# Fused two-block decoder on one core: memory normed in rows, cross-attention blocks interleaved with its heads, differential and sparse attention reordered

## What is computed

```python
# first block
x = x + 0.5 * swiglu(rms_norm(x, ffn1_norm), ...)
x = x + token_mixing(rms_norm(x, mix_norm), ...)          # ends in ... @ w_out
x = x + memory_cross_attention(rms_norm(x, xattn_norm), rms_norm(mem, mem_norm), w_q, w_kv, w_o)
x = x + 0.5 * swiglu(rms_norm(x, ffn2_norm), ...)

def memory_cross_attention(h, m, w_q, w_kv, w_o):         # 512 tokens, 256 memory rows, 4 heads of 256
    q = to_heads(h @ w_q, XATTN_HEADS)
    k, v = (to_heads(t, XATTN_HEADS) for t in jnp.split(m @ w_kv, 2, axis=-1))
    s = jnp.einsum('bhsd,bhmd->bhsm', q, k)
    p = jax.nn.softmax(s * (XATTN_HEAD_DIM ** -0.5), axis=-1)
    return einsum('bhsm,bhmd->bhsd', p, v) reshaped @ w_o

# diff_attention: 8 heads of two 64-wide halves, chunk-causal mask, four query tiles each
p = jax.nn.softmax(jnp.where(mask, s, -jnp.inf), axis=-1)
a = p[:, :, 0] - lam * p[:, :, 1]                         # then a @ v, rms_norm, @ w_out

# dsa_attention: 16 heads of 64, keys chosen per query by an 8-head index score
score = jnp.einsum('bqh,bqhk->bqk', wb, jax.nn.relu(dots))
vals, idx = lax.top_k(score, topk)                        # topk = 128 of up to 512
s = jnp.einsum('bqhd,bqkhd->bhqk', qb, kg); p = softmax(...)
```

## Time and profile before

| | |
|---|---|
| Time, three runs | median 2615.61 us (2611.15 to 2618.03) |
| The profiled execution | 2619.21 us, its span 2617.2 us |
| Granted TensorE clock, mean | 0.962 of full speed |
| TensorE busy | 93% of the span |
| GpSimd, ScalarE, VectorE busy | 43%, 33%, 32% |
| Bytes moved | 210.65 MB, mean 80 GB/s |

### The profile page before, as it was taken

How to read it: one execution, slowest core, us unless ns; L and a number is a source line. 1 busy time by engine, 2 the same in 40 slices (tenths; PEclk the granted TensorE clock), 3 DMA queues, 4 the chain that set the end, 5 groups by cost and what they waited for, 6 DMA issues and landing times.

```text
span 2617.2 us, 27065 instructions
## 1 busy us (share of the span) xinstructions
PE 2444.0 (93%) x11184; PEld 1970.7 (75%) x11184; DVE 845.6 (32%) x1441; ACT 863.4 (33%) x1255; POOL 1124.2 (43%) x918
## 2 busy tenths in 40 slices
PE   7999998898886999999998789999998979999999
PEld 6888876687764788888885477888875757788887
DVE  3222106463123222210455724112045955420211
ACT  4222224221432322221444534213245353431331
POOL 6444433523631544444352236445454711444442
PEclk8999999899899999999898899999999979999999
DMA  4332222212410233322221013233221200232322
GB/s 129 98 98 99 97 97 68 65 52 77 145 65 16 81 97 97 97 97 97 81 81 64 1 49 97 97 97 97 97 77 56 89 1 17 81 97 97 97 97 81
DMA packets 148588, 210.65 MB, mean 80 GB/s; under 512 B 6122, under 2 KB 116979, under 8 KB 148467
## 3 DMA queue, kind: packets, MB, share of 16 engines
q1 hardware_dynamic: 148466, 208.93, 24.6%
HBM read 206.82 MB, written 2.10 MB: 80 GB/s over the span
## 4 chain that ended last, share of the span: by engine, by line
PE 79%; DVE 10%; ACT 4%; POOL 3%; issue 2%; DMA 1%; SPq 0%; ACTq 0%; POOLq 0%; DVEq 0%
PE ps L1254 24%; PE ps L1256 23%; PE ps L1255 23%; POOL wlo L720 2%; PE ps L1879 2%; POOL sq L733 1%; DVE c_work L2542 1%; PE ps L1855 1%; DVE c_best L2541 1%; ACT whi L815 1%; DVE small L2406 1%; ACT d_p L1067 1%; PE ps L1865 1%; PE ps L1543 1%; PE ps L1308 1%
## 5 line engine op out<-in xcount | busy, mean ns | idle before, releaser
L720 POOL TENSOR_TENSOR wlo<-raw,whi 128x512 fp32r<-128x512 f32 x776 | 1011.6, 1336 | 1320.9 <-ACT whi L815 1320.9
L815 ACT ACTIVATE whi<-raw 128x2048 fp32r<-128x2048 f32 (+1 forms) x195 | 371.1, 1904 | 769.1 <-DMA raw<-in_mlp_w 326.2
L1254 PE MATMUL ps<-hh,whi 128*128 128x512 f32 x1512 | 599.6, 397 | 24.6 <-DVE hl L1984 17.3
L1256 PE MATMUL ps<-hh,wlo 128*128 128x512 f32 x1512 | 592.9, 392 | 0.0
L1255 PE MATMUL ps<-hl,whi 128*128 128x512 f32 x1512 | 592.7, 392 | 0.0
L1254 PEld LDWEIGHTS ps<-hh,whi 128*128 128x128 f32 x1512 | 286.7, 190 | 99.0 <-issue 33.6
L1256 PE MATMUL ps<-gh,wlo 128*128 128x512 f32 x864 | 336.1, 389 | 0.0
L1254 PE MATMUL ps<-gh,whi 128*128 128x512 f32 x864 | 336.1, 389 | 0.0
L1255 PE MATMUL ps<-gl,whi 128*128 128x512 f32 x864 | 336.1, 389 | 0.0
L1255 PEld LDWEIGHTS ps<-hl,whi 128*128 128x128 f32 x1512 | 287.1, 190 | 60.0 <-issue 1.5
L1256 PEld LDWEIGHTS ps<-hh,wlo 128*128 128x128 f32 x1512 | 286.3, 189 | 60.5
(11 more groups left out here) (406 smaller groups left out, 2669.9 us busy)
## 6 DMA issues: line engine op xcount, KB each, us to landing
raw<-in_mlp_w SPq DMA_DIRECT2D x64, 1024.0 KB, 5.5
raw<-in_ffn_w_gate SPq DMA_DIRECT2D x22, 1024.0 KB, 5.1
raw<-in_ffn_w_up SPq DMA_DIRECT2D x22, 1024.0 KB, 5.1
raw<-in_ffn_w_down SPq DMA_DIRECT2D x22, 1024.0 KB, 4.8
raw<-in_w_in SPq DMA_DIRECT2D x13, 1024.0 KB, 5.1
raw<-in_diff_w_in SPq DMA_DIRECT2D x12, 1024.0 KB, 5.0
raw<-in_xattn_w_kv SPq DMA_DIRECT2D x8, 1024.0 KB, 5.6
raw<-in_dsa_w_in SPq DMA_DIRECT2D x8, 1024.0 KB, 5.1
```

Of the source, the lines that this page charges most:

```text
L720: nc.gpsimd.tensor_tensor(wlo[i][:, c], raw[i][:, c], whi[i][:, c].bitcast(F32), ALU.subtract).then_inc(s_lo, 1)
L815: nc.scalar.activation(whi[i][:, 0:width(made[0])], raw[i][:, 0:width(made[0])], ACT.Copy)\
L1254: nc.tensor.matmul(dst, w_hi, x_hi, start=start, stop=False)
L1256: return nc.tensor.matmul(dst, w_lo, x_hi, start=False, stop=stop)
```

## The change

**Cross-attention.** The memory is loaded behind the first block of the mixer's out-projection, normed in rows on ScalarE (two squares with a running sum, two scaled copies of 128 x 1024) between two weight preparations, and turned by TensorE in two groups of eight transposes between out-projection blocks 0, 1 and 2. The tokens are no longer normed before the queries: `hh`, `hl` are made from `xT` times the gain, tile by tile as the out-projection's sums arrive, GpSimd adds the squares (`x_sums`), and the token's factor goes into the scale of the exponent (`xqr`). The blocks' order is `X_ORDER`; scores, turns and weighing stand between blocks. The result has buffers of its own (`x_oh`, `x_ol`), so that `hh` and `hl` are free for the next entry. The norm N_X is gone, and the indices of the entries are shifted.

**Differential attention.** The bank pair of a unit is `slot(u)`, scores and exponents of unit 0 move ahead of the last half group of the projection, VectorE does `weights(u + 1)` before `max_(u + 3)`, and the out-projection does the first six feature tiles of blocks 0 and 1 before the last two heads' outputs are turned.

**DSA.** The squares of the query rows are two of 128 x 2048 after the index-score loop, where before there were eight of 128 x 512 beside the copies; VectorE has four rounds of `top(1)` ahead of the first `stats`, and the rotations stand between rounds 10 of `top(3)` and its last six.

```diff
+X_ORDER = ("k0", "k1", "q0", "k2", "q1", "k3", "q2", "v0a", "v0b", "q3", "v1a", "v1b")
+        def slot(u):
+            return (u + 2) % 3
 # SyncE
-                    sp.wait_ge(s_x, 8 * at["x"][1])
+                    load(b, up_src(wdram["w_out"])(0))
+                    sp.wait_ge(s_mvar, GH)
                     sp.dma_start(x_mrow[:, :, :], ...)
...
 # TensorE, end of the mixer
-                project_out(b + MIX_BLOCKS, upd, lambda k: (s_mfin, k + 1), m_hi, m_lo)
+                out_part(b + MIX_BLOCKS, 0, (s_mfin, 1), m_hi, m_lo)
+                pe.wait_ge(s_xmn, MT)
+                turn_memory(0)
+                out_part(b + MIX_BLOCKS, 1, (s_mfin, 1), m_hi, m_lo)
+                pe.wait_ge(s_xml, 4)
+                turn_memory(4)
...
 # ScalarE, out-projection of the mixer and after
+                prep_to(o + 1)
+                act.wait_ge(s_memrow, 16)
+                for m in range(MT):
...
+                    nc.scalar.activation(sq[...], x_mrow[:, m, :], ACT.Square,
+                                         accum_out=xmr[:, m:m + 1]).then_inc(s_xmsq, 1)
+                act.wait_ge(s_xmvar, 1)
+                rsqrt(xmr[:, 4:6], xmr[:, 2:4], s_xmrstd)
+                act.wait_ge(s_xmr, 1)
+                for m in range(MT):
+                    nc.scalar.activation(x_mrow[:, m, :], x_mrow[:, m, :], ACT.Copy, scale=xmr[:, 4 + m:5 + m])
+                prep_to(o + 2)
...
 # VectorE, differential attention
                 weights(0)
-                weights(1)
                 for u in range(32):
-                    if u < 30:
-                        weights(u + 2)
+                    if u < 31:
+                        weights(u + 1)
                     if u < 29:
                         max_(u + 3)
 # TensorE, its out-projection
+                    out_part(out, 0, (s_dhl, 1), o_h, o_l, 0, 6)
+                    out_part(out, 1, (s_dhl, 1), o_h, o_l, 0, 6)
                     turn_out(6, 32)
                     turn_out(7, 32)
 # VectorE, DSA
                 turned_by(0, c_rowa)
+                top(1, 0, 4)
                 stats(1, c_sq0, G_Q0)
                 stats(2, c_sq1, G_Q1)
-                top(1)
+                top(1, 4)
                 stats(3, a_sq, G_K1)
                 top(2)
+                top(3, 0, 10)
                 turned_by(1, c_rowb)
                 turned_by(2, c_rowc)
-                top(3)
                 turned_by(3, c_rowa)
+                top(3, 10)
```

More of the change, by code:

```diff
@@ L457, in two_blocks @@
         s_csum = sem("s_csum")
+        s_csq = sem("s_csq")
         s_cny = sem("s_cny")
@@ L1041, in diff, with exponents @@
                 act.wait_ge(s_rr, 1)
+                def exponents(u):
+                    nk = P * (u % 4 + 1)
+                    act.wait_ge(s_dmax, u + 1)
+                    if u >= 3:
+                        act.wait_ge(s_da, u - 2)
+                    for c in range(2):
+                        k = 2 * slot(u) + c
+                        nc.scalar.activation(d_p[:, u % 3, c, 0:nk], ps[:, k, 0:nk], ACT.Exp,
+                                             bias=small[:, k:k + 1], scale=-1.0, accum_out=small[:, 12 + k:13 + k])\
+                            .then_inc(s_de, 1)
                 for g in range(6):
@@ L1087, in high @@
                         .then_inc(s_dh, 1)
-                for u in range(3):
+                for u in range(1, 3):
                     exponents(u)
@@ new lines, in xattn @@
+                pe.wait_ge(s_x, x0 + 2)
+                keys(0)
+                pe.wait_ge(s_x, x0 + 4)
+                keys(1)
+                pe.wait_ge(s_eacc, acc_at(E_X) + 7)
+                pe.wait_ge(s_x, x0 + 8)
+                for st in range(ST):
+                    r = nc.tensor.matmul(ps[:, 7, 2 * st:2 * st + 2], sq[:, 0, ts(st, P)], ones[:, 0:2],
+                                         start=True, stop=True)
+                r.then_inc(s_ess, 1)
+                queries(0)
@@ new lines, in xattn @@
+                pe.wait_ge(s_xk, 2)
+                keys(2)
+                pe.wait_ge(s_ehalf, E_X + 1)
+                scores(0)
+                pe.wait_ge(s_xk, 4)
+                queries(1)
+                pe.wait_ge(s_xk, 6)
+                keys(3)
+                scores(1)
+                queries(2)
+                pe.wait_ge(s_xk, 8)
+                values(0, 0)
+                pe.wait_ge(s_xe, 4)
+                scores(2)
+                values(0, 1)
+                queries(3)
@@ new lines, in xattn @@
+                pe.wait_ge(s_xv, 2)
+                values(1, 0)
+                pe.wait_ge(s_xe, 8)
+                scores(3)
+                pe.wait_ge(s_xe, 12)
+                turn(0)
+                values(1, 1)
+                turn(1)
+                weigh(0)
+                turn(2)
+                pe.wait_ge(s_xe, 16)
+                weigh(1)
+                turn(3)
+                weigh(2)
+                weigh(3)
+                out = b + X_BLOCKS
+                pe.wait_ge(s_xv, 4)
@@ L1566, in row_group @@
+                out_part(out, 0, (s_xol, 1), x_oh, x_ol, 0, 6)
+                out_part(out, 0, (s_xol, 1), x_oh, x_ol, 6, KT)
+                for j in range(1, OUT_BLOCKS):
+                    out_part(out, j, (s_xol, 1), x_oh, x_ol)
             def row_group(b, r0, xh, xl, kt, wcols, blocks, ready=None):
@@ L1621, in diff, with scores @@
                 half_group(b + 1, 0, 1, (2, 3))
+                def scores(u):
+                    h, qt = divmod(u, 4)
+                    if u == 0:
+                        pe.wait_ge(s_rtc, 16)
+                    if u >= 3:
+                        pe.wait_ge(s_de, 2 * (u - 3) + 2)
+                    for c in range(2):
+                        rows = slice(64 * c, 64 * c + 64)
+                        r = nc.tensor.matmul(ps[:, 2 * slot(u) + c, 0:P * (qt + 1)],
+                                             a_qT[rows, h, ts(qt, P)], a_kT[rows, h, 0:P * (qt + 1)],
+                                             start=True, stop=True)
+                    r.then_inc(s_ds, 1)
                 for g in range(1, 6):
@@ L2534, in dsa, with top @@
                 dv.link(V.memset(c_bias[0:CH, P - CH:P], -NEG))
-                def top(qt):
+                def top(qt, first=0, last=TOPK // 8):
                     c = slice(off[qt], off[qt] + P * (qt + 1))
-                    for r in range(TOPK // 8):
+                    for r in range(first, last):
                         src = c_work if r else c_score
```

477 lines of the change are left out of this document (274 added, 203 removed).

## The result

The changed kernel takes a median of 2513.7 us (2508.87 to 2518.11, four runs) against 2616.82 for the kernel before; the ratio is 0.9603, with a 95% interval from 0.9571 to 0.9636. The profiled execution took 2515.9 us, with a span of 2514.2; 2515 was forecast.

What follows compares the result with a forecast made beforehand. TensorE, busy 93% of the span, was taken as the bound, with gains mainly in its idle time. Cross-attention 73.9, differential attention 15 and DSA 12 sum to 100.9 us, giving 2515 us, range 2498 to 2545.

Steps and rivals of the forecast that it cites:

- The front: Cross-attention: the memory's norm delays the mixer's out-projection, 5.2 us lost; differential attention: unit 0's earlier scores and exponents, 2.3 gained.
- The entry's chain of GpSimd's additions: Entry of ffn2: the sum matmul comes 13.3 us behind the cross-attention's out-projection instead of 15, 1.7 us gained.
- Rival 1: Cross-attention: thin covers fail as GpSimd's splits slow to 6.7 us a block beside VectorE; about 2523 us, chance 0.12.
- my 14: Differential attention's loop: weights one unit further behind remove VectorE's wait for exponents, 14 us gained over seven heads.
- The out-projection's term: Differential attention's end: out-projection halves hold two blocks open and add a hand-over, 1.0 us lost.
- Rival 2: Differential attention keeps its pace, through TensorE's lower clock or larger hand-overs; +13 us, 2528, chance 0.13.
- The rotations: DSA: the six steps of `c_rowb` move to where GpSimd is idle, 5.8 us gained.
- the last turn: DSA: turn of the last keys, copies and first scores run beside the selection's last six rounds, 5.4 us gained.
- the squares: DSA: six squares of 0.5 us leave the chain of score copies, the two large ones hide; 2.5 us gained.
- the bound from TensorE's and GpSimd's chain: DSA: blocks, turns and copies allow first exponents only at 2096.8 to 2100 instead of 2110, 10 to 13.3 us gained.
- rival 3: DSA wins only its last term because TensorE and GpSimd come last there; +6.6 us, 2521, chance 0.12.
- rival 4: Cross-attention's dense stretch: the granted clock falls, up to +165.5 us, giving 2680, so slower than before; chance 0.03.

## Why the prediction was right

- **Cross-attention, 73.9 for 74.9.** The sum of TensorE's work stands: 165 us without a gap. The front was priced at 5.2 and cost 4.3; the small steps were longer than I put them, 3.3 for 1.8, with two of them at 0.71 and 1.19 beside GpSimd's split, but TensorE's part was shorter. The two errors happened to offset each other. The entry's chain of GpSimd's additions ended the stretch, as said, 14.0 us behind the out-projection for the forecast 13.3. Rival 1 did not happen: the splits took 5.0 us a block in the dense stretch, and no block waited. In the run with the heads behind the blocks two blocks did wait, but with splits of 5.0 us as well: the covers are thin, as predicted, and the slower splits of the rival appeared in neither run.
- **Differential attention, 15 for 15.0, by terms that were partly wrong.** The loop with the front undone is worth 14.6 (99.8 in the kernel with the cross-attention alone, 85.2), which is my 14. The front is worth 1.0 at most, not 2.3, and none of that in the loop: the step that failed is that one unit's head start would move the loop, which from the second unit on it hardly does. The out-projection's term, booked as 1.0 lost, gains 2.7. The edits are not additive here: undone one by one they cost 15.8, 1.0 and 2.7, all undone at once (the cross-attention alone) 14.4. That the sum came out at 15.0 is luck in part. Rival 2's condition, TensorE at its lower level, held in part for the first three heads. They took 12.0, 11.4 and 12.5 us where the others took 11.3, so it cost some 2 us and not the rival's 13.
- **DSA, 12 for 13.0.** Front 11.9. The rotations cost 7.5 where I had 5.8, the last turn 4.5 where I had 5.4, the squares 0.9 where I had 2.5 (six times 0.5 is 3.0, and the prediction gives no reason for its 2.5). I took 12 instead of the sum of 13.7 because of the bound from TensorE's and GpSimd's chain, first exponents at 2096.8 to 2100 in the old trace's time. TensorE's first scores came at 2096.2 in that time (2006.19 and the shift of 90.0 us at the MLP's sum); with the 1.3 us that lay between them and the first exponents before (2108.78 to 2110.09) that chain allowed first exponents at 2097.5. They came at 2098.2, behind VectorE's masked scores. So the bound was right in size but did not decide, nor did rival 3; the 11.9 come from terms that were off by 0.9 to 1.7 each, and agree with the 12 in part by luck. The heads' 1.1 us were not in the sum.
- **No fall of the clock in the dense stretch** (rival 4): 1.00 over 165 us.

What carried the forecast was that each wait removed had work to be replaced by, and that this work could be added up from rows at full clock. Where it failed in size, it was mostly the meeting of VectorE with GpSimd or the granted clock, which the sum did not have.

## What to carry to other kernels

Where one engine is nearly always busy, write down its work behind the change as one list and look for the covers under a microsecond or two; scores or turns put between weight blocks both hide a softmax and feed the engine that prepares the blocks. In a loop in which two engines take turns, a step set one unit further behind was worth the whole wait here. A later stage whose instructions are the same can be longer or shorter by up to 10 us with another granted clock, so compare stage by stage before an edit is credited or blamed.

## What the runs showed of the hardware

- DSA's heads took from 100.8 to 111.1 us for the same instructions, with granted clocks from 0.98 to 0.87, and the same length the one time that each of two programs was traced again (111.1 twice, 110.1 twice; 100.8 in two kernels with the small squares, 102.2 in one without). Why the lower level falls where it does stays open, and so does whether it can differ between executions of one program.
- A TENSOR_SCALAR of 128x256 on VectorE took 1.32, 2.54 or 6.33 us beside GpSimd's run of splits, and the longest ended within 0.3 us of that run's end. The one of 1.32 ended 0.14 us behind the end of the piece that it had started beside (1951.41), while the run went on. It has one SBUF input, so what I cited in the prediction for two inputs does not cover it; the Trainium skill (GPSIMD Engine Reference, section 1 Specifications) names a second case of contention, VectorE's instructions in a 2-port mode. That the row belongs to this case was not tested.
- The rotation steps, with two SBUF inputs, took 0.42 alone and up to 1.5 beside GpSimd, in whichever half of the twelve the two met. Steps over only two columns took 0.71 and 1.19 us beside a split, and the next one, behind it, 0.16.
